# A latent attention whose rotated keys lie in two padded images

## What is computed

```python
a = h @ w_a
cq, ckv, kr = jnp.split(a, [Q_LORA, Q_LORA + KV_LORA], axis=-1)
q = (rms_norm_2(cq, g_q) @ w_uq).reshape(B, S, MLA_HEADS, NOPE_DIM + ROPE_DIM)
q_nope = q[..., :NOPE_DIM]
q_rope = apply_rope(q[..., NOPE_DIM:], cos[:, :, None], sin[:, :, None])
kv = (rms_norm_2(ckv, g_kv) @ w_ukv).reshape(B, S, MLA_HEADS, NOPE_DIM + V_DIM)
k_nope, v = kv[..., :NOPE_DIM], kv[..., NOPE_DIM:]
k_rope = apply_rope(kr, cos, sin)
...
s = (jnp.einsum('bqhd,bkhd->bhqk', qn, k_nope, preferred_element_type=jnp.float32)
     + jnp.einsum('bqhr,bkr->bhqk', qr, k_rope, preferred_element_type=jnp.float32)) * scale
```

## Time and profile before

| | |
|---|---|
| median of 3 runs | 1090.29 us |
| lowest, highest | 1088.93, 1090.34 us |
| span of the profiled execution | 1086.7 us |
| TensorE (PE) busy | 1073.5 us, 99% |
| VectorE (DVE) busy | 740.5 us, 68% |
| ScalarE (ACT) busy | 560.8 us, 52% |
| GpSimd (POOL) busy | 40.2 us, 4% |
| mean granted TensorE clock | 0.999 |

### The profile page before, as it was taken

The page is one execution under the profiler, slowest core; times in us unless marked ns, Lnnn a source line. Parts: engine busy times, 40 slices in busy tenths (PEclk is TensorE's granted clock), DMA queues, the critical chain, the costliest instruction groups (busy, mean ns, idle before and its releaser), DMA issues.

```text
span 1086.7 us, 15287 instructions
## 1 busy us (share of the span) xinstructions
PE 1073.5 (99%) x5810; PEld 908.4 (84%) x5810; DVE 740.5 (68%) x1044; ACT 560.8 (52%) x723; POOL 40.2 (4%) x59
## 2 busy tenths in 40 slices
PE   8999999999999999999999999999999999999997
PEld 6888888888888888888878888888889778888886
DVE  5756665656686656568877975665897878666665
ACT  5556444435455444346665544445653766444453
POOL 1000000000000000000000220000300300000000
PEclk9999999999999999999999999999999999999999
DMA  9953366564547564637532755657576324754651
GB/s 332 338 168 116 92 218 212 155 217 169 171 148 236 179 207 158 228 106 204 176 110 78 237 191 195 193 165 255 156 237 228 92 79 156 232 185 163 206 180 39
DMA packets 127162, 195.83 MB, mean 180 GB/s; under 512 B 6977, under 2 KB 97217, under 8 KB 126994
## 3 DMA queue, kind: packets, MB, share of 16 engines
q1 hardware_dynamic: 123904, 185.77, 51.8%
q0 software_dynamic: 3216, 9.51, 3.0%
q10 hardware_dynamic: 2, 0.00, 0.0%
HBM read 194.21 MB, written 1.05 MB: 180 GB/s over the span
## 4 chain that ended last, share of the span: by engine, by line
PE 95%; DVE 3%; ACT 1%; issue 1%; DVEq 0%; DMA 0%; ACTq 0%
PE ps L2099 25%; PE ps L2000 15%; PE ps L2002 15%; PE ps L2001 15%; PE ps L2102 13%; PE ps L2181 2%; PE ps L2220 1%; PE ps L2042 1%; PE ps L2597 1%; PE ps L2183 1%; DVE act L1237 1%; PE ps L2246 1%; PE ps L2595 1%; PE ps L2632 1%; PE ps L2279 1%
## 5 line engine op out<-in xcount | busy, mean ns | idle before, releaser
L2099 PE MATMUL ps<-act,whi 128*128 128x512 f32 x1200 | 424.4, 397 | 0.0
L1112 DVE TENSOR_TENSOR wlo<-raw,whi 128x2048 fp32r<-128x2048 f32 (+2 forms) x161 | 363.9, 2277 | 87.5 <-ACT whi L672 87.1
L2102 PE MATMUL ps<-act,wlo 128*128 128x256 f32 x1200 | 336.7, 281 | 0.0
L672 ACT ACTIVATE whi<-raw 128x2048 fp32r<-128x2048 f32 (+2 forms) x170 | 317.6, 1887 | 26.7 <-PE ps L2002 20.6
L2099 PEld LDWEIGHTS ps<-act,whi 128*128 128x128 f32 x1200 | 225.2, 188 | 53.7
L2102 PEld LDWEIGHTS ps<-act,wlo 128*128 128x128 f32 x1200 | 226.7, 189 | 2.0
L2002 PE MATMUL ps<-whi,hlo 128*128 128x512 f32 x400 | 157.1, 393 | 0.0
L2000 PE MATMUL ps<-whi,hhi 128*128 128x512 f32 x400 | 156.7, 392 | 0.1
L2001 PE MATMUL ps<-wlo,hhi 128*128 128x512 f32 x400 | 156.6, 392 | 0.0
L2000 PE MATMUL ps<-whi,act 128*128 128x512 f32 (+2 forms) x286 | 112.4, 393 | 1.5 <-DVE act L1812 0.6
L2002 PE MATMUL ps<-whi,act 128*128 128x512 f32 (+2 forms) x286 | 108.0, 378 | 0.0
(11 more groups left out here) (230 smaller groups left out, 1154.5 us busy)
## 6 DMA issues: line engine op xcount, KB each, us to landing
raw<-mlp_w_up_in SPq DMA_DIRECT2D x32, 1024.0 KB, 6.5
raw<-mlp_w_down_in SPq DMA_DIRECT2D x32, 1024.0 KB, 4.9
raw<-ffn_w_gate_in SPq DMA_DIRECT2D x22, 1024.0 KB, 5.4
raw<-ffn_w_up_in SPq DMA_DIRECT2D x22, 1024.0 KB, 5.3
raw<-ffn_w_down_in SPq DMA_DIRECT2D x22, 1024.0 KB, 4.9
raw<-attn_w_qkv_in SPq DMA_DIRECT2D x10, 1024.0 KB, 9.2
raw<-w_kv_shared_in SPq DMA_DIRECT2D x8, 1024.0 KB, 5.3
raw<-attn_w_o_in SPq DMA_DIRECT2D x4, 1024.0 KB, 5.0
```

Of the source, the lines that this page charges most:

```text
L672: nc.scalar.activation(whi[:, s, 0:width], raw[:, s, 0:width], ACT.Copy).then_inc(hi_ready, 1)
L1112: nc.vector.tensor_tensor(wlo[:, s, 0:width], raw[:, s, 0:width], whi[:, s, 0:width].bitcast(F32), ALU.subtract).then_inc(lo_ready, 1)
L2099: nc.tensor.matmul(bank(b + f), lhsT=w[0][:, at:at + P], rhs=act[:, k, :, :].rearrange("p a t -> p (a t)"), start=k == 0, stop=False, skip ...
L2102: ins = nc.tensor.matmul(bank(b + f, 0, T), lhsT=w[1][:, at:at + P], rhs=act_hi[:, k, :], start=False, stop=k == KT - 1, skip_group_check= ...
```

## The change

The rotated keys get two images of 128 partitions by 256 tokens, `kr_padded[:, 0, :]` with the keys in partitions 0 to 63 and zeros in the others, and `kr_padded[:, 1, :]` with the keys in partitions 64 to 127 and zeros below. The second score product takes all 128 partitions of `qrT`, which hold two heads, against the image whose zeros remove the other head. GpSimd writes the zeros in two instructions ahead of the load of the row `pre0`, after a wait for the last pooling product, since the images reach into the place of `band`. ScalarE copies the keys of each tile in two halves of 64 partitions, one into each image. TensorE waits for the zeros once, ahead of `keys_up(0)`.

```diff
-        krT = arena[:, 3456:3712]
+        kr_padded = arena[:, 3456:3968].rearrange("p (e t) -> p e t", e=2)
...
+        kr_cleared = sem("kr_padding_cleared")
...
             for name in ROWS[1:ROW["fpost0"] + 1]:
+                if name == "pre0":
+
+                    pool.wait_ge(pooled, 4)
+                    nc.gpsimd.memset(kr_padded[64:128, 0, :], 0.0).then_inc(kr_cleared, 1)
+                    nc.gpsimd.memset(kr_padded[0:64, 1, :], 0.0).then_inc(kr_cleared, 1)
                 load_row(name)
...
                 if k1 == 6:
-                    nc.scalar.activation(krT[:, t * P:(t + 1) * P], bank(b, n * P, (n + 1) * P), ACT.Copy)\
-                        .then_inc(kr_copied, 1)
+                    for e in range(2):
+                        part = slice(64 * e, 64 * (e + 1))
+                        ins = nc.scalar.activation(kr_padded[part, e, t * P:(t + 1) * P],
+                                                   ps[part, b * HALF + n * P:b * HALF + (n + 1) * P], ACT.Copy)
+                    ins.then_inc(kr_copied, 1)
...
             pe.wait_ge(kr_copied, 2)
+            pe.wait_ge(kr_cleared, 2)
...
             def mla_score(h, t, o):
                 nc.tensor.matmul(o, lhsT=qT[:, h, t * P:(t + 1) * P], rhs=kT[:, h, keys(t)], start=True, stop=False)
-                lo = 64 * (h % 2)
-                return nc.tensor.matmul(o, lhsT=qrT[lo:lo + 64, h // 2, t * P:(t + 1) * P],
-                                        rhs=krT[lo:lo + 64, keys(t)], start=False, stop=True)
+                return nc.tensor.matmul(o, lhsT=qrT[:, h // 2, t * P:(t + 1) * P],
+                                        rhs=kr_padded[:, h % 2, keys(t)], start=False, stop=True)
```

## The result

The changed kernel takes 1083.9 us, the median of 5 runs (1083.11 to 1084.15), against 1090.0 us (5 runs, 1088.93 to 1090.34) before: ratio 0.9944, 95% interval 0.9933 to 0.9955. The span of the profiled execution is 1082.1 us, 4.6 us less than before and 0.1 us from the 1082.0 of the sum. So the stage did what the prediction said, and the median fell further than the stage explains.

The account below looks back on a forecast made before the run. TensorE, busy 99% of the span, was taken to bound the kernel. 5.5 - 0.5 - 0.15 - 0.1 = 4.7 us gave span 1082.0, and with 3.6 us around it 1085.6 us, 0.43% faster; range 1084.0 to 1088.0.

Parts of the forecast that it names:

- Second product on 128 rows: Latent attention scores on TensorE: eight heads take 10.5 us instead of 16.0, 5.5 us less.
- Why the loss was the alternation: Latent scores: the lost time comes from changing between 64 and 128 rows, not from f32, accumulation or 64 rows.
- Wait for the low part: Ahead of head 2's second keys, TensorE waits for VectorE's conversion of the weight chunk: 0.5 us lost.
- VectorE behind at the last head: Normalising the last probabilities in the latent attention: VectorE late by 0.15 us, bounds 0 and 1.2 us.
- Copies of the keys: ScalarE's half-tile copies of rotated keys delay TensorE's turning of the queries: 0.1 us, bounds 0 and 0.3.
- Clearings: GpSimd's two zero writes after the pooling products: 0 us lost, bounds 0 and 0.5 us.
- Sum of the stage: Latent attention gain after waits: 5.5 - 0.5 - 0.15 - 0.1 = 4.7 us, span 1082.0 us.
- 3.6 us lie around the span and stay: Profiled span 1086.7 us against median 1090.29: the 3.6 us difference was taken as fixed outside the span.
- The range: Whole kernel's time: 1084.0 to 1088.0 us, from no wait taking anything back to VectorE's rival at 2 us.
- rows do not matter: Rival for the latent scores: the pauses belong to something the change keeps; 1090.4 us, chance 0.09.
- Weight loads in the open: Rival for the latent scores: 128-row weight loads no longer hide beside products; 6.5 us more, 1096.8 us, chance 0.04.
- VectorE taking the gain back: Rival in the latent attention: VectorE falls behind and TensorE waits, 1 to 3 us; 1086.6 to 1088.6 us, chance 0.10.

Follow-up runs that it names:

- again: The changed kernel timed once more with no edit: 1084.41 us, ratio 0.9950.
- the images alone: Changed kernel with its images, clearings and waits, but the second score product on 64 rows again: 1089.99 us, ratio 1.0001.
- the rows without images: Kernel before with the second score product on all 128 rows of the old key tile, unpadded, the other head's product left in: 1084.71 us, ratio 0.9952.
- the products all on 64 rows: Kernel before with the first score product also on 64 rows, half of each head's own key columns left out: 1086.23 us, ratio 0.9966.
- The grouped products: Kernel before with each head's products reordered, both 128-row ones and then both 64-row ones: 1086.61 us, ratio 0.9970.
- two heads at a time: Kernel before, no images, two heads' 128-row products, then their four 64-row products in alternating halves: 1084.67 us, ratio 0.9955.

## Why the prediction was right and wrong, point by point

- *Second product on 128 rows, 5.5 us:* right. Eight heads take 8 x 1.31 = 10.5 us. What was not in the sum: the turning of the probabilities behind a 64-row product cost 0.38 us from start to start (547.49 to 547.87 in the trace of before), behind a 128-row one 0.33 (563.49 - 563.16); for the six heads that have it there, 0.3 us more. The first key product behind head 1 cost 0.23 (537.41 to 537.64) where 0.12 is usual: 0.1 more.
- *Why the loss was the alternation:* right, and shown by two changes of rows a head (1.59 us) and by none (1.31 us) in kernels without images, and by products all of 64 rows, which do not pause among themselves. The Trainium skill's rule that few rows last as long as 128 ("TensorE: Matmul & The Clock Gate", section "Why this matters for your kernels") holds for products of equal rows (1.50 us with the ends, 1.31 without); it says nothing of the change between them, which is what cost.
- *Wait for the low part, 0.5 us:* right in place and near in size, 0.62 us, 0.69 with the longer product behind it. The prediction let the conversion stand still; it moved 0.5 us later (534.15 to 534.67) with the turning of the queries, and the scores moved as much.
- *VectorE behind at the last head, 0.15 us:* smaller. TensorE turns the last probabilities at 569.32 us, 2.42 behind the turning before it, where the trace of before has 2.38 (571.65 to 574.03): about 0.04 us late. VectorE's idle time ahead of the latent attention's maxima is 0.62 us in all, under the 2 us named.
- *Copies of the keys, 0.1 us:* too low; 0.33 us at the turning alone, and 0.45 to 0.49 in all by the stages with and without the images, well over the bound of 0.3. The mis-sized term is the copy of 64 partitions, put at 0.15 us after the neighbour of 128 partitions; the first pair holds ScalarE for 0.56 us, 0.28 each. The chosen price was the distance from a 128-partition copy to the instruction behind it; the upper bound, the printed duration of 0.27, was nearer the truth. It went through the second split (526.36, start forecast for 526.0) and the rotation into TensorE's wait. The first keys were not quite covered either: the split ends at 526.78, the keys start at 526.86, and their second product comes 0.20 us later, not 0.12.
- *Clearings, 0 us:* right. Two of 0.31 us; a wait of 3.23 us ahead of them for the pooling products; the row is loaded 4.05 us later (303.06 to 307.11), and nobody waits for it.
- *Sum of the stage, 4.7 us:* right, in part by luck: 5.5 + 0.3 + 0.1 - 0.69 - 0.45 - 0.04 = 4.7 us from the measured terms, 4.75 measured, span 1082.1 for 1082.0. Two errors (0.4 us of gain not counted, 0.4 us of waits too low) cancel.
- *"3.6 us lie around the span and stay":* this is the step that failed. The forecast of 1085.6 us missed by 1.7, of which 0.3 are the median of before, 1090.0 with five runs instead of 1090.29 with three. Only 1.9 to 2.1 us lie around the span. The other 1.6 us were the distance between a quick execution, the profiled one, and the usual one, and this part did not stay: usual spans went from 1088.1 us to 1082.0 (first result) and from 1088.2 to 1082.5 us (again), 5.7 to 6.1 us. Of these, 4.75 are the stage. 0.3 lie at the end: from the issue of the last output write to the end of the span it is 1086.7 - 1083.30 = 3.4 us before and 1082.1 - 1078.98 = 3.1 after, 3.1 also with the images alone, and 3.4 in the rows without images; why the images shorten it is open. The 0.6 to 1.1 us that are left fit one gated-FFN loop that goes at the mixed pace instead of 16.79 us throughout: the usual span before is that of two loops at 16.79 (1086.6 for the mean of the three without, and 0.7 to 0.9 for each: 1088.0 to 1088.4), the usual one after that of one. For the edited kernels the traces of median executions show one such loop. For the kernel before this is argued, not shown: its usual executions were not traced, and those traced with one such loop took 1089.6 us, 0.4 to 0.7 less than its medians.

Timelines of SyncE's queue for the end of the span, before and then after:

```profile
1083.30 0.99 SPq L543 DMA_DIRECT2D y_out<-x  x2
```
```profile
1078.98 0.99 SPq L544 DMA_DIRECT2D y_out<-x  x2
```

- *The range:* its low end took the largest gain of the stage (5.5 us) and 0.7 us of scatter, and so rested on the same frame. A range that let 1.6 us of the difference between the profiled execution and the median go or stay would have held 1083.9.
- *The rivals:* rows do not matter, refuted by the changed kernel, the rows without images and the products all on 64 rows: the same two pairs of operands take turns there, without pauses. The grouped products (3.4 us less) halve the changes of rows and the turns of the operands alike, and so do not tell the two apart. Weight loads in the open, refuted by the loads after the change; the loads without a lead over their products were those at the changes of rows, in the kernel before. VectorE taking the gain back did not happen in the changed kernel, and did happen with two heads at a time.

## What to carry to other kernels

Where f32 products of 64 and of 128 rows alternate on TensorE, count the changes, at about 0.19 us each here, before counting rows: pad to one size, or group products of one size (padding took 0.7 us off a head's 2.0; pairing the halves took 0.9, but asked VectorE for two heads at once). When a stage becomes shorter, look one engine further for what stood just in time: two moves in VectorE's order gave another 0.97 us in the stage. And set the profiled execution's time beside the median before building a forecast on its span: if it is not the median, find where the two differ (here mostly in the pace of two loops) before taking the difference as fixed.

## What the hardware showed that was not expected

- Copies of 64 partitions by 128 columns out of PSUM follow one another at 0.28 us, twice the 0.15 us after which a 256-column copy started behind a 128-partition one; half the partitions saved nothing. Why they took longer is open.
- An iteration of the gated-FFN loops lasts either 16.59 or 16.80 us, with the same number of instructions and a granted clock of 1.00, in turns or, in some executions, 16.79 throughout. What decides is open.
- The last output write ends 0.3 us sooner behind its issue in the kernels that hold the images: 3.1 us to the end of the span in all four traces with them, 3.4 to 3.5 in the nine without.
- At a change between 64 and 128 rows the weight load starts with its product (533.65 and 533.66 us); between products of equal rows it starts 0.11 us ahead (533.97 and 534.08).
